# Seven projection units of the first chunk advanced together, one block of h at a time

## What is computed

```python
mod = jax.nn.silu(c) @ w_ada + b_ada
shift, scale, gate = jnp.split(mod, 3, axis=-1)
h = _layer_norm(x) * (1 + scale[:, None]) + shift[:, None]
proj = h @ w_in
xa, ga, u, v, gb = jnp.split(proj, SPLITS, axis=-1)
ya = _pool_mixer(xa, w_pool, pool_scale) * jax.nn.silu(ga)
yb = _sgu_mixer(gelu(u), gelu(v), sgu_ln_g, sgu_ln_b, w_sgu, b_sgu) * jax.nn.silu(gb)
y = jnp.concatenate([ya, yb], axis=-1) @ w_out
z = DEEPNORM_ALPHA * x + gate[:, None] * y
return _layer_norm(z) * ln_g + ln_b
```

## Time and profile before

| what | us |
|---|---|
| median of 3 runs | 690.5 |
| lowest and highest | 687.81, 692.12 |
| profiled execution, its time | 691.21 |
| its span, first to last instruction | 689.3 |
| PE busy | 666.3 |
| DVE busy | 548.4 |
| ACT busy | 250.1 |

### The profile page before, as it was taken

One profiled execution on the slowest core, in us unless ns is written; L12 is line 12 of the kernel. 1 busy time (PEld: TensorE's weight loads), 2 busy tenths in 40 slices (PEclk: granted clock), 3 DMA queues, 4 the chain that ended last, 5 costly groups with the idle time before them and its releaser, 6 DMA issues.

```text
span 689.3 us, 8811 instructions
## 1 busy us (share of the span) xinstructions
PE 666.3 (97%) x3069; PEld 553.9 (80%) x3069; DVE 548.4 (80%) x1000; ACT 250.1 (36%) x334; POOL 66.3 (10%) x75
## 2 busy tenths in 40 slices
PE   8779999999999999999999999999999999998995
PEld 7668888877888888887888888888888888887885
DVE  5967779969879978866969978776987987656676
ACT  4446333316522433234722343332821343323300
POOL 2001101110002201100002201000002210000010
PEclk9999999999999999999999999999999999999998
DMA  8934575395334362288343562388343454224011
GB/s 337 379 124 152 175 284 183 97 206 218 123 106 138 123 244 95 90 121 306 104 142 97 178 233 72 110 76 315 114 148 112 141 192 166 92 94 171 11 61 62
DMA packets 33978, 106.68 MB, mean 155 GB/s; under 512 B 6514, under 2 KB 7570, under 8 KB 33940
## 3 DMA queue, kind: packets, MB, share of 16 engines
q1 hardware_dynamic: 33940, 106.22, 48.7%
HBM read 97.80 MB, written 8.40 MB: 154 GB/s over the span
## 4 chain that ended last, share of the span: by engine, by line
PE 87%; DVE 5%; DMA 4%; issue 2%; ACT 1%; SPq 0%; POOLq 0%; POOL 0%; DVEq 0%; ACTq 0%
PE bank_b L887 59%; PE bank_a L887 24%; DMA w_float<-in_w_units 2%; DVE v_gelu L565 2%; PE bank_a L981 1%; DMA x_norm<-in_x 1%; DVE w_low L525 1%; PE bank_a L983 1%; PE bank_b L938 0%; ACT h_high L423 0%; DVE h_low L530 0%; ACT w_high L408 0%; PE bank_b L964 0%; PE bank_b L963 0%; DVE v_gelu L563 0%
## 5 line engine op out<-in xcount | busy, mean ns | idle before, releaser
L887 PE MATMUL bank_b<-h_high,w_high 128*128 128x512 f32 x512 | 201.0, 393 | 0.0
L887 PE MATMUL bank_b<-h_high,w_low 128*128 128x512 f32 x512 | 199.4, 389 | 0.0
L887 PE MATMUL bank_b<-h_low,w_high 128*128 128x512 f32 x512 | 199.4, 389 | 0.0
L408 ACT ACTIVATE w_high<-w_float 128x1024 fp32r<-128x1024 f32 x108 | 113.9, 1056 | 149.0 <-DMA w_float<-in_w_units 75.6
L525 DVE TENSOR_TENSOR w_low<-w_float,w_high 128x1024 fp32r<-128x1024 f32 x108 | 131.6, 1220 | 43.5 <-ACT w_high L408 43.0
L887 PEld LDWEIGHTS bank_b<-h_high,w_low 128*128 128x128 f32 x512 | 96.1, 188 | 20.4
L887 PEld LDWEIGHTS bank_b<-h_low,w_high 128*128 128x128 f32 x512 | 96.2, 188 | 19.7 <-issue 0.2
L887 PEld LDWEIGHTS bank_b<-h_high,w_high 128*128 128x128 f32 x512 | 96.1, 188 | 19.8 <-issue 0.2
L359 POOL TENSOR_TENSOR z_rstd<-z_var_eps,minus_half 128x1 f32<-128x1 f32 x16 | 22.0, 1378 | 360.8 <-DVE z_var_eps L750 350.9
L887 PE MATMUL bank_a<-w_high,y_high 128*128 128x512 f32 x128 | 50.1, 392 | 3.2 <-DVE gate_b L684 1.8
L887 PE MATMUL bank_a<-w_high,h_high 128*128 128x512 f32 x128 | 50.9, 398 | 1.0 <-DVE w_low L525 1.0
(11 more groups left out here) (156 smaller groups left out, 953.2 us busy)
## 6 DMA issues: line engine op xcount, KB each, us to landing
w_float<-in_w_units SPq DMA_DIRECT2D x108, 512.0 KB, 3.4
z<-in_mod_units SPq DMA_DIRECT2D x20, 512.0 KB, 6.1
x_norm<-in_x SPq DMA_DIRECT2D x16, 512.0 KB, 4.7
z<-in_x SPq DMA_DIRECT2D x16, 512.0 KB, 5.4
out<-z SPq DMA_DIRECT2D x15, 512.0 KB, 4.8
x_norm<-in_x_channels SPq DMA_DIRECT2D x12, 512.0 KB, 14.8
x_norm<-in_w_units SPq DMA_DIRECT2D x4, 512.0 KB, 6.3
v_gelu<-token_rows SPq DMA_DIRECT2D x6, 256.0 KB, 8.1
```

The source lines that it names most:

```text
L408: nc.scalar.activation(wH[:, n % S_SLOTS, :], wF[:, n % F_SLOTS, :], ACT.Copy).then_inc(w_high, 1)
L887: last = mm(bank, wl if n == 2 else wh, ml if n == 1 else mh, start=start and n == 0, stop=stop and n == 2)
```

## The change

In chunk 0 seven units, the four of v and xa, ga, u of group 0, advance together: when a block of h is there, each unit that can use it does its part of it (v 12 matmuls, the others 3 each). The order in which the units' weights are made is EARLY; they get slots and landing places of their own, among them the first half of the v parts (vH, vL) as a fifth slot and gate_rows as a third landing place. The first two blocks of h have column blocks of their own in the modulation (two blocks of weights each), and PE multiplies five blocks, not two. The x tiles are loaded ahead of the modulation blocks; POOL makes the offsets of three x tiles, DVE normalises the fourth itself. h's high part is made before its float copy.

The bias of the spatial mixer is one product of ones with the turned weights, and DVE puts scale and bias to it per head (before: eight small products and an evacuation). DVE's work on the branches of group 0 and on v stands in a list of its own (first_branches), and the loops of chunk 0 begin at step 8. The pooled and spatial products of chunk 0 have places of their own (FIRST_POOL_AFTER and so on), the gate sums begin one step later. In all chunks three waits are added: ACT's tanh of ga waits for gb_gated, DVE's two gates wait for yp_ready and ys_ready of the group before.

```diff
+FIRST_POOL_AFTER = (8, 11, 14, 18)
+FIRST_SGU_AFTER = (10, 11, 14, 17)
+EARLY = (0, 1, 4, 5, 6, 2, 3, 7)
...
-GATE_SUM_FROM = 9
+GATE_SUM_FROM = 10
...
-PE_MODS = (0, 1)
+PE_MODS = (0, 1, 2, 3, 4)
...
-WARM_UP = (22, 1, 3, 0, 4)
+WARM_UP = (18, 6)
```

SP's first loads, ACT's list after the first h blocks, DVE's list, and PE's:

```diff
+            load_m(0)
+            load_m(1)
+            load_early(0)
+            for m in range(2, 8):
+                load_m(m)
+            load_early(1)
+            load_early(4)
+            load_early(5)
+            load_m(8)
+            load_m(9)
+            load_early(6)
+            for m in range(10, 13):
+                load_m(m)
+            load_early(2)
+            for m in range(13, MOD_COLS):
+                load_m(m)
+            load_early(3)
...
+            small_weights()
+            act.wait_ge(unit_done, V_UNITS)
+            for j in range(TILES):
+                nc.scalar.activation(gv[:, j, :], A[:, j, :], ACT.Gelu).then_inc(v_gelu, 1)
+            act.wait_ge(unit_done, V_UNITS + 1)
+            nc.scalar.activation(X[:, HALO:], B[:, 0, :], ACT.Copy).then_inc(xa_copied, 1)
+            split_high(0, FIRST_LOOP)
...
+            dve.wait_ge(x_rstd, TILES)
+            vec.tensor_scalar(xn[:, TILES - 1, :], xn[:, TILES - 1, :], xmv[:, TILES - 1, 0:1],
+                              xrs[:, TILES - 1:TILES], ALU.subtract, ALU.mult).then_inc(x_last, 1)
+            mod_cols_of(0)
+            early_low(0)
+            h_split(0, 0)
+            mod_sum(5)
+            mod_cols_of(1)
+            mod_sum(6)
+            h_split(0, 1)
+            mod_sum(7)
+            early_low(1)
+            mod_cols_of(2)
...
+            def first_branches(c):
+
+                sgu_bias()
+                v_stats_of(c, 0)
+                pooling(c, 0, True)
+                split_low(c, FIRST_LOOP)
+                v_stats_of(c, 1)
+                pooled_low(c, 0)
+                gate(ga_tanh, ga_gated, sga, 1, 1)
+                split_low(c, FIRST_LOOP + 1)
+                v_norm_of(c, 0)
+                v_stats_of(c, 2)
+                v_norm_of(c, 1)
+                v_stats_of(c, 3)
+                small_weights()
+                v_norm_of(c, 2)
+                v_low_of(c, 0)
+                v_norm_of(c, 3)
+                for j in range(1, TILES):
+                    v_low_of(c, j)
...
-                for h in range(G):
-                    cut = slice(h * P, (h + 1) * P)
-                    mm(B[:, 3, cut], sgubB[:, cut], wtF[:, cut], start=True, stop=False)
-                    last = mm(B[:, 3, cut], ones[0:1, :], bsgu_row[:, cut], start=False, stop=True)
-                last.then_inc(e_done, 1)
+                mm(B[:, 3, :], ones[:, :], wtF, start=True, stop=True).then_inc(e_done, 1)
...
+            turn_x(4)
+            early_channel(ga, (3,))
+            early_channel(u, (0, 1, 2, 3))
+            early_high_passes(4)
+            turn_x(5)
+            early_low_pass(4)
+            early_channel(xa, (4,))
+            early_channel(ga, (4,))
+            early_channel(u, (4,))
...
-                        if n in POOL_AFTER:
-                            if first and n == POOL_AFTER[0]:
+                        if n in pool_after:
+                            if first and n == pool_after[0]:
                                 pe.wait_ge(small_low, 2)
-                            pool_product(c, POOL_AFTER.index(n))
+                            pool_product(c, pool_after.index(n))
```

More of the change, by code:

```diff
@@ L223, in run_chunks, with places, early_bank, early_w @@
             chunk(CHUNKS - 1, False, True)
+        def places(first):
+            if first:
+                return FIRST_POOL_AFTER, FIRST_SGU_AFTER, FIRST_MIX_IN, FIRST_YS_IN
+            return POOL_AFTER, SGU_AFTER, MIX_IN, YS_IN
+        def early_bank(k):
+            return (0, 2)[k] if k < 2 else 3
+        def early_w(unit):
+            s = EARLY_SLOT[unit]
+            if s == SPARE_SLOT:
+                return tuple(t[:, 0:2, :].rearrange("p a b -> p (a b)") for t in (vH, vL))
+            return wH[:, s, :], wL[:, s, :]
+        def early_float(unit):
+            i = EARLY_LANDING[unit]
+            return gateB[:, :] if i == SPARE_LANDING else wF[:, i, :]
+        def w_of(c, n):
+            if isinstance(c, int) and c == 0 and n in EARLY:
+                return early_w(n)
+            return wH[:, n % S_SLOTS, :], wL[:, n % S_SLOTS, :]
         def m_sem(m):
@@ L264, in _ @@
                 sp.dma_start(xn[:, j, :], x_tiles[0, j]).then_inc(xn_landed[j], 16)
[L265 to L277, removed]
-                    sp.dma_start(bsgu_row, b_sgu).then_inc(small_landed, 16)
+            load_m(0)
@@ L645, in small_weights, with sgu_bias @@
                     .then_inc(small_low, 1)
+            def sgu_bias():
+                dve.wait_ge(e_done, 1)
+                dve.wait_ge(small_high, 2)
+                for h in range(G):
+                    cut = slice(h * P, (h + 1) * P)
+                    last = vec.scalar_tensor_tensor(out=E[:, h, :], in0=B[:, 3, cut], scalar=halfc[:, 2 * G + h:2 * G + h + 1],
+                                                    in1=bsguB[:, cut], op0=ALU.mult, op1=ALU.add)
+                last.then_inc(e_ready, 1)
             def pooling(c, g, first):
@@ L765, in chunk @@
                     x_steps.begin(c + 1)
-                for n in range(IN_UNITS + 1 if last else UNITS):
-                    if not (last and n in LAST_SPLITS_IN) and not (first and n + AHEAD < V_UNITS):
+                pool_after, sgu_after, mix_in, ys_in = places(first)
+                if first:
+                    first_branches(c)
+                for n in range(FIRST_LOOP if first else 0, IN_UNITS + 1 if last else UNITS):
+                    if not (last and n in LAST_SPLITS_IN):
                         split_low(c, n + AHEAD)
@@ L889, in product, with token_unit @@
                 return last
-            def token_unit(s, q, tiles, banks, actH, actL, j_order=range(TILES), parts=(0, 1),
-                           passes=(0, 1, 2)):
+            def token_unit(w, q, tiles, banks, actH, actL, j_order=range(TILES), parts=(0, 1), passes=(0, 1, 2)):
                 for j in j_order:
@@ L1046, in chunk @@
             def chunk(c, first, last):
-                for n in range(IN_UNITS if last else UNITS):
-                    s = n % S_SLOTS
+                pool_after, sgu_after, _, _ = places(first)
+                for n in range(V_UNITS + len(EARLY_CHANNEL) if first else 0, IN_UNITS if last else UNITS):
+                    w = w_of(c, n)
                     pe.wait_ge(w_low, c * UNITS + n + 1)
```

413 lines of the change are left out of this document (264 added, 149 removed).

## The result

The changed kernel takes 693.31 us (median of 7 runs, 692.02 to 695.4), the kernel before 690.5: the ratio is 1.0044, with an interval of 1.0025 to 1.0063. It is slower by some 3 us, which is within 1%. The profiled execution took 692.02 us, 690.3 of them its span, and is the fastest of the seven; that of before took 691.21. So the two profiles lie only 0.8 us apart.

The account below looks back on a forecast made before the run. DVE bounds until 48 us, then PE; the front's 9.5 us go into waits of 4.2 and 4.4 and 0.5 elsewhere, becoming 1.8 lost: 691.2 + 1.8 = 693.0, less 0.7 gives 692.3 us; range 686 to 699.

Parts of the forecast that it names:

- The front: First chunk's start: seven units done at 68.0 instead of 77.5, a gain of 9.5 us.
- The first hold: PE before the first pooled product: waits 4.2 us, to 83.1, for DVE's small splits.
- DVE's list: DVE from v's first GELU tile to the third group's pooled split: 68.2 to 123.3, taking back the front's 9.5 us.
- The second hold: PE at the third pooled product: arrives at 119.5 and waits 4.4 us for DVE.
- the part on the clock: Clock falls behind PE's two gaps, paid from the second wait and 2.0 us spare; otherwise 3 more, 695.3; 6 in 100.
- The output units: Start at 159.0, 1.8 us late, set by DVE's split of unit 18 and the load of unit 21; PE there at 157.0.
- The rival in which the gain stays: DVE's 8.1 us of waits serve as reserve, PE never holds, time 681.0; 9 in 100.
- The load rival: SP's queue between 88 and 125: late weight loads add 6.0 us to DVE's list, time 698.3; 12 in 100.

Follow-up runs that it names:

- e1: Changed kernel with DVE's two small splits moved early, right behind the first gate of ga; 694.16 us, ratio to before 1.0049.
- e2: Changed kernel with DVE's gate sums of blocks 1 and on cut to 8 of 1024 columns; 692.6 us, ratio 1.0019.
- h1: Changed kernel unaltered, run again beside a later experiment on the same chip; 695.51 us, ratio 1.0034.
- f1: Changed kernel with chunk 0's token row stores and four x_channels tiles moved behind the load of unit 21; 693.48 us, ratio 1.0037.
- f2: Changed kernel with gate sums cut to 8 columns and the token row stores moved behind the load of unit 21; 689.94 us, ratio 0.9981.
- e3: Changed kernel with both small splits early and gate sums cut to 8 of 1024 columns; 693.88 us, ratio 1.0027.
- g3: Changed kernel with shorter early DVE list, token rows first, unit 21 held back, gate product behind unit 23, nothing left out; 692.58 us, ratio 0.9994.
- g4: Like g3, but with the last gate sums moved into DVE's lull in steps 13 to 18; 687.32 us, ratio 0.9924.

## Why the prediction was right

The forecast was 692.3 us, and no measurable difference; measured 693.31, 1.0 us more, inside the range. For the profiled execution the forecast was 693.0, and 692.0 was measured, 1.0 us less; that it is as close as this on both sides is in part luck, as the last step below shows. The path was, step by step:

- **The front.** Forecast 50.6 us of work from 15.4 and 2.0 of waits. The wait at the second column sum was 1.8 for 1.7. The seven units were done at 69.0, not 68.0: the third modulation block of PE started at 16.05, since its first had waited 1.1 us for a load, which the forecast left out, and the rest took 0.4 us longer. This 1.0 us runs through the later places.
- **The first hold.** Forecast 4.2 us, released by the small splits; measured 4.0, by w_pool_low, at 84.54.
- **DVE's list.** Forecast 68.2 to 123.3, 55.1 us; measured 69.42 to 124.13, 54.7, of which 2.0 are waits. Right as a sum, and right as the cause: e1 moved PE's stalls along the list and the time stayed, e2 shortened the list and the third product came without a wait, and in the kernel before the same cut gave nothing.
- **The second hold.** Forecast 4.4, measured 2.6. Of the 1.8 us between them the fall of the clock behind the first hold took some 1.3 (PE's work from there to the third pooled product took 37.7 us for 36.4), as the part on the clock allowed for; the rest is that the first hold ended 1.4 us late and DVE's list only 0.8. That the two falls cost nothing up to the fourth pooled product is shown by the filled gaps. The rule of the Trainium skill that was weighed ("TensorE: Matmul & The Clock Gate", "HAM oscillation — how this bites in real kernels") has each long gap make the next burst of matmuls start at the half clock. Here the granted clock fell behind both gaps, of 4.0 and 2.6 us; in the second profiled execution it fell behind the first, of 4.0, and not behind the second, of 1.7.
- **The output units.** Forecast 159.0, measured 159.4, and that they agree is partly luck. This step failed as it was put: "PE itself is there at 157.0, so this wait decides". The wait was where the forecast had it: y_pool and the gate rows were ready before 158.8. But PE came last, 2.4 us later than forecast, and had no wait there. Rows of PE's, ACT's and DVE's timelines:

```profile
151.40 0.50 PE L1041 MATMUL bank_a<-pooled_high,w_pool_high 128*128 128x512 f32 x1 [0.34 <-DVE pooled_low L808]
...
157.69 0.60 ACT L610 ACTIVATE gate_rows<-bank_b 128x512 f32<-128x512 f32 x1
...
158.01 0.75 DVE L821 SCALAR_TENSOR_TENSOR y_pool<-bank_a,half_cols,gate_a 128x512 f32<-128x512 f32 x1
...
159.39 0.39 PE L1041 MATMUL bank_a<-w_high,y_high 128*128 128x512 f32 x1
```

0.9 us of it came with the third pooled product, some 1.5 from the second fall of the clock, and 0.3 from a wait at the fourth pooled product, less 0.3 that the forecast had to spare. DVE's low part for that one ended at 151.35, held up by something the forecast did not have (the last section), and without the fall PE waits 2.0 us for it. The load of unit 21 is a second bound within 2 us. In h1 it decides, as the forecast had it, but later: from its issue to ACT's part of it went 16.4 us instead of 13.8, and PE waited 2.04 us for the gate rows behind it:

```profile
158.09 1.06 ACT L484 ACTIVATE w_high<-w_float 128x1024 fp32r<-128x1024 f32 x1 [11.49 <-DMA w_float<-in_w_units]
```

```profile
161.28 0.47 PE L1041 MATMUL bank_a<-w_high,y_high 128*128 128x512 f32 x1 [2.04 <-ACT gate_rows L610]
```

That moving the load alone gave nothing (f1) and that it took back what a shorter DVE list gave (e2 against f2) fit two bounds so close together.

The rival in which the gain stays needed DVE's 8.1 us of waits as a reserve. DVE did use it: 2.0 us of waits are left, and its stretch shrank from 62.7 to 54.7 us. But it began 10.0 us later (59.45 to 69.42), so the pooled split of the third group came 2.0 us later than before, at 124.13 for 122.15. The load rival had the right mechanism at the wrong place: before 130 DVE waited for no split by more than 0.6 us, but the load behind the token rows was late for e2 and e3, which came there sooner.

## What to carry to other kernels

An engine that is 86% busy beside the bound one had no room here for a list that starts 10 us later: before a front is moved up, ask what the next engine's list is worth back to back, and take as much off it as the front gives. When a cure moves no time, look for the wait that took its place and cure both before judging either; here four places stood in a row (DVE's list, the load behind the token rows, the centring behind them, GpSimd's addition), and a cure of some of them measured as nothing. Work that is put off has to be put into a lull that the timeline shows, not merely later.

## What the runs showed of the hardware

GpSimd's addition of the gate bias works on one partition and 1024 columns and takes 2.4 to 3.5 us. A DVE instruction that begins beside it is stretched by 0.9 to 2.2 us. In the changed kernel, POOL's timeline and DVE's:

```profile
147.56 3.23 POOL L458 TENSOR_TENSOR gate_rows<-gate_rows,z 1x1024 f32<-1x1024 f32 x1 [11.43 <-DVE gate_rows L754]
```

```profile
148.47 2.88 DVE L808 TENSOR_TENSOR pooled_low<-sum_a,pooled_high 128x512 fp32r<-128x512 f32 x1
```

The same instruction takes 0.68 us elsewhere (124.13 above). In the kernel before the addition ran from 138.34 and met a copy of 16 columns, 2.37 us instead of 0.17, at a place where nobody waited; the change moved it by 9 us onto the low part that PE waits for. In g3 it met an h split (2.83), in g4 the split of unit 21 (2.47 instead of 1.22). It is in all fourteen traces, and the stretched instruction ends behind the addition by no more than it takes elsewhere. That the one causes the other was not tried by itself. The Trainium skill ("SBUF — State Buffer", section "SBUF: two separate sides") says that GpSimd and certain DVE instructions, those with two SBUF inputs among them, take a pair of ports by an exclusive lock for a whole instruction, so that the other one waits rather than shares. The rows above fit that: the low part, which reads two SBUF tiles, ends 0.56 us behind the addition and takes 0.68 us by itself.

The DMA engines moved little while the token rows' two stores of 2 KB were under way: 112 GB/s at a share of 1.01 in 138 to 148 us, then 314 at 0.91 in 148 to 158. In these rows (length, busy time of five engines, clock, DMA share, GB/s) they stand with the DMA issues behind them; the four tiles of x_channels took a median of 13.1 us, where the 107 weight loads of the same size have 3.4 over the span.

```profile
138.00:148.00 10.00, 10.00 (x50) 8.43 (x49) 9.66 (x16) 4.36 (x6) 0.44 (x1) 1.00 1.01 112
148.00:158.00 10.00, 9.66 (x39) 7.03 (x38) 6.49 (x6) 2.23 (x4) 2.79 (x1) 1.00 0.91 314
```

```profile
w_float<-in_w_units SPq DMA_DIRECT2D x107, 512.0 KB, 3.4
...
x_norm<-in_x_channels SPq DMA_DIRECT2D x4, 512.0 KB, 13.1
```

That the small stores are what slows the others was not tried by itself.

A way to bring the next chunk's mean and rstd to all partitions without these stores was not tried; the chain of a store of 8.5 to 14 us and a load of 7 to 9 stands in every trace, and whether it is what bounds chunk 0 in g4 was not tried.
